# A two-block transformer kernel on one core: sums of squares for the norms, spread over DVE, ACT and TensorE in another way

## The chip, the cores and the metric

The kernel runs on 1 core of one Trainium2 chip. The time is device time in microseconds (us); of several runs the median is given. The engines are TensorE (PE in the profile; PEld are its weight loads), VectorE (DVE), ScalarE (ACT), GpSimd (POOL) and SyncE (SP, which issues the DMAs of the weights).

## The reference

A sequence of 512 tokens with 1024 channels goes through two blocks. What matters here are the RMS norms between the parts:

```python
def rmsnorm(x, g):
    xf = x.astype(jnp.float32)
    y = xf * lax.rsqrt(jnp.mean(xf * xf, axis=-1, keepdims=True) + RMS_EPS)
    return (y * g.astype(jnp.float32)).astype(x.dtype)

# first block, two layers (pooling mixer, then gated mixer "sgu")
x = x + g1 * mixer(modulate(rmsnorm(x, norm_mix_g[i]), sh1, sc1))
x = x + g2 * square(relu(modulate(rmsnorm(x, norm_mlp_g[i]), sh2, sc2) @ w1)) @ w2
x = rmsnorm(x, final_g)

# second block, one layer
h = rms_norm(x, norm_mix_pre)
proj = h @ w_in                          # q, k, v and the inputs of the recurrence
mix = concat(attention(q, k, v), rwkv7_time_mix(...)) @ w_out
x = x + rms_norm(mix, norm_mix_post)
f = conv_gated_ffn(rms_norm(x, norm_ffn_pre), w_ffn_up, conv_w, conv_b, w_ffn_down)
x = x + rms_norm(f, norm_ffn_post)
```

Inside `rwkv7_time_mix` the decays are `exp(-exp(w_log))` with `w_log` from `tanh(zw) @ w_decay_up`, and the rates of a are `sigmoid(a0 + za @ w_iclr_up)`.

## The kernel before

The activations lie transposed: channels on the 128 partitions in eight tiles (`xT[:, 0..7]`), the 512 tokens along the free axis. Every linear layer is worked off in slabs of 512 x 512 weights. DMA brings a slab to `raw`; ACT copies its rounded high part to `w_hi` (`split_to`, line 1140), DVE takes the low part `w_lo` as the difference (line 1568); TensorE makes 16 tile products of three matmuls each (`slab`, line 531). Two slabs are held at a time. The product of a group of slabs fills four PSUM banks, one for each tile of 128 outputs; a bank is evicted as soon as it is full, by DVE or ACT, while TensorE fills the next.

The order on each engine is that of its own program, written out by hand: `tensor_program`, `scalar_program`, `vector_program`, `gpsimd_program` and `sync_program`. They meet in counting semaphores. There is no planner.

A norm runs as follows. ACT squares the eight tiles (`square`, line 1158), each into one of four places of `squares`: tile 0 into place 3, the others in turn into places 0 to 2. DVE adds each to place 3 (`add_square`, line 1595), so seven additions make the sum over tiles. TensorE sums it over the partitions (`norm_mean`, line 542): for each 128 tokens the sum is loaded as the stationary operand, and one column of 1/1024 runs through it, so that the mean of each token comes to a partition of bank 4. ACT takes the root (`root`, line 1162), DVE the reciprocal and a diagonal matrix (`inverse_and_diagonal`, lines 1583 and 1585), TensorE spreads it over all partitions (`norm_spread`, line 547), and DVE and ACT scale the tiles and split them in high and low parts, for which the first slab of the next layer waits.

The norms are named after their place: `NORM_MIX0` before the pooling mixer (its additions are on POOL), `NORM_MLP0` before the first MLP, `NORM_MIX1` behind it, `NORM_MLP1` after `sgu_out`, `NORM_FINAL` after the second MLP, `NORM_POST` after `w_out`, `NORM_FFN` before the feed-forward, `NORM_LAST` behind it. Where squares come from a layer with two groups of output tiles, the additions of tiles 1 to 3 are made while the second group is multiplied, and those of tiles 4 to 7 after the last eviction. At `NORM_POST`, ACT evicts the banks to `mixed` (line 1502) and squares tiles 4 to 7 from there after the last of them. At `NORM_FFN` the squares are those of `xT` as DVE makes it, tile by tile, from `mixed` (lines 2201 and 2205); one addition stands in each step of that loop from the third on.

In the projection of the second block (`proj`, five pairs of slabs) other matmuls stand between the slabs. After the first slab of the second pair comes `decays` on TensorE (line 757), which waits for `first_copied`: a copy by ACT (line 1374) of the spread of `NORM_FINAL` out of bank 5. Four matmuls of the same shape follow later, `rates` (line 763).

## Time and profile before

| | |
|---|---|
| runs, us | 2003.49, 1999.51, 2000.14 (median 2000.14) |
| profiled execution, us | 2002.35, its span 2000.9 |
| mean granted TensorE clock in it | 0.941 of full speed |
| PE busy | 1825.2 us, 91% |
| PEld busy | 1473.2 us, 74% |
| DVE busy | 1052.0 us, 53% |
| ACT busy | 645.0 us, 32% |
| POOL busy | 82.5 us, 4% |

The span goes from the first to the last instruction of the profiled execution; the 1.45 us beside it lie around them. Busy shares of different engines overlap. TensorE's granted clock stands at one of two levels, 1.00 (2.4 GHz) or 0.50 (1.2 GHz); a stretch with both has a value between. An fp32 matmul leaves two records each of PE and PEld.

### The profile page before, as it was taken

What the parts mean: (1) busy time and instruction counts of PE and PEld (TensorE: products, weight loads), DVE (VectorE), ACT (ScalarE), POOL (GpSimd) and SP (SyncE); (2) the same over time, 40 slices, a digit from 0 to 9 for tenths busy, and PEclk for the clock granted to TensorE, in tenths of its full rate; (3) what the DMA queues carried; (4) which work ended last, traced back from release to release, by engine and by line L of the source; (5) the groups of instructions that cost most, each with busy time, mean ns of one, the idle gap of its engine ahead of it and who ended that gap; (6) DMA issues with size and microseconds to landing.
All of it is one profiled execution on the core that took longest, in us unless ns stands there. A gap on an engine that the chain in (4) does not pass through costs nothing.

```text
span 2000.9 us, 21459 instructions
## 1 busy us (share of the span) xinstructions
PE 1825.2 (91%) x8828; PEld 1473.2 (74%) x8828; DVE 1052.0 (53%) x1336; ACT 645.0 (32%) x796; POOL 82.5 (4%) x87
## 2 busy tenths in 40 slices
PE   4659999999896899999999989976599999999997
PEld 2238888888685688888886868855388888888885
DVE  4874675477426544234356574444565642456533
ACT  2123312322322243123244523332244431344412
POOL 2400010000000000000000101000000000000000
PEclk8769999999897899999998989987699999999997
DMA  9713474366230232323322240002123323232321
GB/s 356 275 64 105 143 236 151 102 209 222 74 105 9 76 105 87 104 88 102 105 90 69 85 100 4 4 1 66 40 85 105 100 90 105 84 105 91 100 84 42
DMA packets 124000, 208.55 MB, mean 104 GB/s; under 512 B 13965, under 2 KB 48421, under 8 KB 123904
## 3 DMA queue, kind: packets, MB, share of 16 engines
q1 hardware_dynamic: 115424, 174.94, 26.7%
q0 software_dynamic: 7808, 29.43, 4.4%
q10 hardware_dynamic: 672, 2.82, 0.4%
q8 instruction: 70, 1.15, 0.2%
q14 instruction: 26, 0.21, 0.0%
HBM read 204.01 MB, written 4.73 MB: 104 GB/s over the span
## 4 chain that ended last, share of the span: by engine, by line
PE 85%; DVE 10%; ACT 2%; DMA 1%; issue 1%; SPq 1%; DVEq 0%; ACTq 0%
PE bank L531 73%; DVE ada_acc L1643 2%; DMA ada_ring<-in_ada_w 1%; PE bank L878 1%; PE bank L547 1%; PE bank L861 1%; PE bank L841 1%; SPq L476 1%; PE bank L542 1%; DVE gT L1969 1%; DVE outer L1967 0%; PE bank L923 0%; PE bank L673 0%; PE bank L902 0%; PE bank L950 0%
## 5 line engine op out<-in xcount | busy, mean ns | idle before, releaser
L1568 DVE TENSOR_TENSOR w_lo<-raw,w_hi 128x2048 fp32r<-128x2048 f32 x138 | 316.2, 2292 | 533.0 <-ACT w_hi L1140 533.0
L1140 ACT ACTIVATE w_hi<-raw 128x2048 fp32r<-128x2048 f32 x138 | 263.8, 1912 | 632.7 <-PE bank L531 609.8
L531 PE MATMUL bank<-u_hi,w_hi 128*128 128x512 f32 x768 | 300.6, 391 | 0.8 <-DVE conv L2225 0.8
L531 PE MATMUL bank<-h_hi,w_hi 128*128 128x512 f32 x736 | 292.8, 398 | 7.9 <-DVE h_lo L1615 7.7
L531 PE MATMUL bank<-u_hi,w_lo 128*128 128x512 f32 x768 | 299.1, 389 | 0.0
L531 PE MATMUL bank<-u_lo,w_hi 128*128 128x512 f32 x768 | 298.9, 389 | 0.0
L531 PE MATMUL bank<-h_lo,w_hi 128*128 128x512 f32 x736 | 289.4, 393 | 0.0
L531 PE MATMUL bank<-h_hi,w_lo 128*128 128x512 f32 x736 | 289.2, 393 | 0.0
L531 PE MATMUL bank<-f_hi,w_hi 128*128 128x512 f32 x512 | 200.4, 391 | 2.4 <-DVE f_lo L1618 2.4
L531 PE MATMUL bank<-f_lo,w_hi 128*128 128x512 f32 x512 | 199.9, 391 | 0.0
L531 PE MATMUL bank<-f_hi,w_lo 128*128 128x512 f32 x512 | 199.8, 390 | 0.0
L531 PEld LDWEIGHTS bank<-h_hi,w_hi 128*128 128x128 f32 x736 | 139.9, 190 | 47.4 <-issue 15.1
L531 PEld LDWEIGHTS bank<-u_hi,w_hi 128*128 128x128 f32 x768 | 144.2, 188 | 31.1 <-DVE conv L2225 1.6
L531 PEld LDWEIGHTS bank<-u_hi,w_lo 128*128 128x128 f32 x768 | 144.2, 188 | 30.4
L531 PEld LDWEIGHTS bank<-u_lo,w_hi 128*128 128x128 f32 x768 | 144.2, 188 | 29.6
L531 PEld LDWEIGHTS bank<-h_hi,w_lo 128*128 128x128 f32 x736 | 140.0, 190 | 29.7
L531 PEld LDWEIGHTS bank<-h_lo,w_hi 128*128 128x128 f32 x736 | 140.3, 191 | 28.8 <-issue 0.5
L531 PEld LDWEIGHTS bank<-f_hi,w_hi 128*128 128x128 f32 x512 | 96.4, 188 | 25.3 <-issue 3.9
L531 PEld LDWEIGHTS bank<-f_hi,w_lo 128*128 128x128 f32 x512 | 96.5, 189 | 20.0
L531 PEld LDWEIGHTS bank<-f_lo,w_hi 128*128 128x128 f32 x512 | 96.6, 189 | 19.9
L1793 DVE SCALAR_TENSOR_TENSOR ada_acc<-ada_ring,c_act,ada_acc 128x256 f32<-128x256 f32 x168 | 81.4, 485 | 6.0
L1525 ACT ACTIVATE conv<-bank,vec 128x512 f32<-128x512 f32 x64 | 50.0, 781 | 104.7 <-PE bank L531 104.7
(351 smaller groups left out, 2040.3 us busy)
## 6 DMA issues: line engine op xcount, KB each, us to landing
raw<-in_mlp_w SPq DMA_DIRECT2D x128, 512.0 KB, 4.6
raw<-in_w_ffn_up SPq DMA_DIRECT2D x64, 512.0 KB, 4.4
ada_ring<-in_ada_w POOLq DMA_DIRECT2D x24, 1024.0 KB, 5.8
ada_ring<-in_ada_w SPq DMA_DIRECT2D x9, 2048.0 KB, 13.9
raw<-in_w_ffn_down SPq DMA_DIRECT2D x32, 512.0 KB, 4.4
raw<-in_w_in SPq DMA_DIRECT2D x20, 512.0 KB, 4.4
raw<-in_sgu_w_in SPq DMA_DIRECT2D x16, 512.0 KB, 4.9
x_rows<-in_ada_w SPq DMA_DIRECT2D x3, 2048.0 KB, 11.8
```

Of the source, the lines that this page charges most:

```text
L476: sy.dma_start(m.ada_slot(g), t["ada_w"][0, :, 512 * g:512 * g + 512] .rearrange("(k p) n -> p k n", p=P)).then_inc(sem(f"ada_in{g % ADA_R ...
L531: mm = te.matmul(bank[:, n], a, b, start=first and k == 0 and j == 0, stop=last and k == 3 and j == 2)
L542: mm = te.matmul(bank[:, 4, j:j + 1], total[:, P * j:P * j + P], m.mean_ones[:, 0:1], start=True, stop=True)
L547: te.matmul(m.rstd_bank, ones[:, :], m.rstd_diag[:, :, :].rearrange("p j t -> p (j t)"), start=True, stop=True).then_inc(sem("spread"), 1)
L841: mm = te.matmul(bank[:, b + i // 2, 256 * (i % 2) + j0:256 * (i % 2) + 256], m.qT[r0:r0 + 64, i, P * n:P * n + P], m.kT[r0:r0 + 64, P * n ...
L861: mm = te.matmul(bank[:, 7, 64 * i:64 * i + 64], m.p_t[:, q, i], m.v_rows[:, n - 1 + q, 64 * half:64 * half + 64], start=q == (n == 0), st ...
L878: mm = te.matmul(bank[:, b + hp, 256 * ii:256 * ii + 256], stationary[rr, i, tok], m.ar[rr, i, :, tok], start=True, stop=True)
L1140: se.activation(m.ring(s)[0], m.raw[:, slot], ACT.Copy).then_inc(sem("hi_made"), 1)
L1525: se.activation(m.conv[:, n], bank[:, n], ACT.Identity, scale=m.col("conv_w_2", 128 + place), bias=m.col("conv_b_2", place)).then_inc(sem( ...
L1568: ve.tensor_tensor(lo, m.raw[:, slot], hi.bitcast(F32), ALU.subtract).then_inc(sem("lo_made"), 1)
L1643: ve.scalar_tensor_tensor(out=a, in0=m.ada_slot(g)[:, k], scalar=m.c_act[:, k:k + 1], in1=a, op0=ALU.mult, op1=ALU.add).then_inc(sem("ada_ ...
L1793: ve.scalar_tensor_tensor(out=a, in0=m.ada1_ring[:, u % 2, kk], scalar=m.c_act[:, kk:kk + 1], in1=a, op0=ALU.mult, op1=ALU.add).then_inc(s ...
```

## The change

The program for each engine is changed by hand:

- After `NORM_MIX1`'s, `NORM_MLP1`'s and `NORM_LAST`'s layers, DVE adds the square of tile `o - 1` right behind the eviction of tile `o`, for tiles 5 to 7, and not all four additions after the last eviction.
- At these three and at `NORM_POST`, the square of tile 7 is no longer added by DVE. It lies in place 0, and `norm_mean` makes four more matmuls from it, which accumulate on the same four columns.
- At `NORM_POST`, ACT squares tiles 4 to 7 directly from their banks, each ahead of the copy that evicts it.
- At `NORM_FFN`, DVE makes no additions. ACT writes the eight squares to eight places, and `norm_mean_of_all` sums them on TensorE, four matmuls for each, which accumulate.
- On ACT, the copy that `first_copied` stands for moves ahead of the split of one slab.
- `NORM_MIX0`, `NORM_MLP0` and `NORM_FINAL` keep their seven additions; only the start flag of the mean's matmuls stands on the first of the four alone, at all norms.

```diff
@@ Python level
-ADDED_ON_DVE = (NORM_MLP0, NORM_MIX1, NORM_MLP1, NORM_FINAL, NORM_POST, NORM_FFN, NORM_LAST)
+ADDED_ON_DVE = (NORM_MLP0, NORM_MIX1, NORM_MLP1, NORM_FINAL, NORM_POST, NORM_LAST)
+LAST_APART = (NORM_MIX1, NORM_MLP1, NORM_POST, NORM_LAST)
+SUMMED_ON_PE = (NORM_FFN,)
+def additions(norm):
+    return 6 if norm in LAST_APART else 7
@@ tensor_program
-    def norm_mean(norm, total):
-        name, count = added(norm, 7)
+    def norm_mean(norm, squares):
+        name, count = added(norm, additions(norm))
         te.wait_ge(sem(name), count)
+        apart = norm in LAST_APART
         for j in range(4):
-            mm = te.matmul(bank[:, 4, j:j + 1], total[:, P * j:P * j + P], m.mean_ones[:, 0:1], start=True, stop=True)
+            mm = te.matmul(bank[:, 4, j:j + 1], squares[:, 3, P * j:P * j + P], m.mean_ones[:, 0:1], start=j == 0, stop=not apart,
+                           skip_group_check=True)
+        if apart:
+            te.wait_ge(sem("squared"), 8 * norm + 8)
+            for j in range(4):
+                mm = te.matmul(bank[:, 4, j:j + 1], squares[:, 0, P * j:P * j + P], m.mean_ones[:, 0:1], start=False, stop=True,
+                               skip_group_check=True)
+        mm.then_inc(sem("meaned"), 1)
+
+    def norm_mean_of_all(norm, squares):
+        for k in range(DT):
+            te.wait_ge(sem("squared"), 8 * norm + k + 1)
+            for j in range(4):
+                mm = te.matmul(bank[:, 4, j:j + 1], squares[:, k, P * j:P * j + P], m.mean_ones[:, 0:1], start=k == 0 and j == 0,
+                               stop=k == DT - 1, skip_group_check=True)
         mm.then_inc(sem("meaned"), 1)
...
-    norm_mean(NORM_POST, squares[:, 3])
+    norm_mean(NORM_POST, squares)
     norm_spread(NORM_POST)
-    norm_mean(NORM_FFN, squares[:, 3])
+    norm_mean_of_all(NORM_FFN, squares)
@@ scalar_program
     def square(norm, k, src, squares):
+        if norm in SUMMED_ON_PE:
+            se.activation(squares[:, k], src, ACT.Square).then_inc(sem("squared"), 1)
+            return
...
     normed_hi(range(4, 8))
-    split_to(first + 3)
     se.wait_ge(sem("spread"), NORM_FINAL + 1)
     se.activation(m.first_rstd, m.rstd_bank, ACT.Copy).then_inc(sem("first_copied"), 1)
+    split_to(first + 3)
     decays()
...
         for n in range(4):
             full(s + 1, group, n)
+            if g:
+                square(NORM_POST, 4 + n, bank[:, n], squares)
             se.activation(m.mixed[:, 4 * g + n], bank[:, n], ACT.Copy).then_inc(sem("act_emptied"), 1)
-    for o in range(4, 8):
-        emptied(GROUPS["w_out"] + 1, o - 4)
-        square(NORM_POST, o, m.mixed[:, o], squares)
@@ vector_program, mlp
                     if layer and half and g:
                         gained_lo(o)
-        for o in range(4, 8):
-            add_square(next_norm, o, sq)
-            if layer:
+                    elif half and g and n:
+                        add_square(next_norm, o - 1, sq)
+        if layer:
+            for o in range(4, 8):
+                add_square(next_norm, o, sq)
                 add_second_square(o)
@@ vector_program, after sgu_out
+            if g and n:
+                add_square(NORM_MLP1, o - 1, m.sq_c)
-    for o in range(4, 8):
-        add_square(NORM_MLP1, o, m.sq_c)
@@ vector_program, after w_out and before the feed-forward
-    for o in range(4, 8):
+    for o in range(4, 7):
         add_square(NORM_POST, o, squares)
...
         ve.tensor_tensor(m.xT[:, k], m.xT[:, k], m.mixed[:, k], ALU.add).then_inc(sem("x_mixed2"), 1)
-        if k >= 2:
-            add_square(NORM_FFN, k - 1, squares)
-    add_square(NORM_FFN, 7, squares)
@@ vector_program, after the last down projection
                     ve.tensor_tensor(m.f[:, o], m.f[:, o], bank[:, n], ALU.add).then_inc(sem("dve_emptied"), 1)
-    for o in range(4, 8):
-        add_square(NORM_LAST, o, m.conv)
+                    if g and n:
+                        add_square(NORM_LAST, o - 1, m.conv)
```

## Rows read from the trace of the kernel before

**Rows 1.** The page: the chain that ended last, shares by engine.
```profile
PE 85%; DVE 10%; ACT 2%; DMA 1%; issue 1%; SPq 1%; DVEq 0%; ACTq 0%
```

**Rows 2.** Timeline at the norm after `sgu_out` (start us, us, engine, line, op, tiles, count, [idle]).
```profile
682.69 0.75 DVE L1858 SCALAR_TENSOR_TENSOR xT<-bank,mod,xT 128x512 f32<-128x512 f32 x1 [1.97 <-PE bank L531]
683.36 3.07 DVE L1595 TENSOR_TENSOR sq_c<-sq_c 128x512 f32<-128x512 f32 x4
...
686.48 1.05 PE L542 MATMUL bank<-mean_ones,sq_c 128*128 128x1 f32 x8 [3.83 <-DVE sq_c L1595]
...
688.82 2.07 PE L547 MATMUL bank<-rstd_diag,ones 128*128 128x512 f32 x2 [1.29 <-DVE rstd_diag L1585]
```

**Rows 3.** Timeline at the norm after the first layer's MLP.
```profile
499.20 0.75 DVE L1761 SCALAR_TENSOR_TENSOR xT<-bank,mod,xT 128x512 f32<-128x512 f32 x1 [1.20 <-PE bank L531]
...
502.99 1.35 PE L542 MATMUL bank<-mean_ones,sq_b 128*128 128x1 f32 x8 [3.04 <-DVE sq_b L1595]
...
505.23 0.21 DVE L1803 TENSOR_TENSOR mod<-bank,vec 128x48 f32<-128x48 f32 x1 [2.30 <-PE bank L673]
```

**Rows 4.** Timeline at the norm after `w_out`.
```profile
1415.61 0.60 ACT L1502 ACTIVATE mixed<-bank 128x512 f32<-128x512 f32 x1 [2.12 <-PE bank L531]
...
1419.89 1.87 PE L542 MATMUL bank<-mean_ones,ar 128*128 128x1 f32 x8 [4.32 <-DVE ar L1595]
1421.80 0.26 ACT L1162 ACTIVATE rstd_rows<-bank,eps 128x4 f32<-128x4 f32 x1 [3.51 <-PE bank L542]
```

**Rows 5.** Timeline at the feed-forward's norm.
```profile
1425.16 0.75 DVE L2201 SCALAR_TENSOR_TENSOR mixed<-mixed,vec,bank 128x512 f32<-128x512 f32 x1 [2.17 <-PE bank L547]
...
1426.56 0.74 DVE L2201 SCALAR_TENSOR_TENSOR mixed<-mixed,vec,bank 128x512 f32<-128x512 f32 x1
1426.67 0.63 ACT L1158 ACTIVATE ar<-xT 128x512 f32<-128x512 f32 x1 [4.61 <-DVE xT L2205]
...
1442.69 0.26 ACT L1162 ACTIVATE rstd_rows<-bank,eps 128x4 f32<-128x4 f32 x1 [2.69 <-PE bank L542]
```

**Rows 6.** Timeline at the last norm.
```profile
1976.68 1.28 ACT L1162 ACT_TABLE_LOAD   x1
...
1978.38 1.87 PE L542 MATMUL bank<-mean_ones,conv 128*128 128x1 f32 x8 [3.77 <-DVE conv L1595]
```

**Rows 7.** Timeline around the decay matmuls.
```profile
1081.20 1.89 ACT L1140 ACTIVATE w_hi<-raw 128x2048 fp32r<-128x2048 f32 x1
...
1083.00 0.58 ACT L1374 ACTIVATE rstd_diag<-bank 128x512 f32<-128x512 f32 x1
1083.12 2.29 DVE L1568 TENSOR_TENSOR w_lo<-raw,w_hi 128x2048 fp32r<-128x2048 f32 x1 [1.04 <-ACT w_hi L1140]
...
1083.72 7.04 PE L757 MATMUL bank<-zT,lora 64*128 64x512 f32 x8 [2.95 <-ACT rstd_diag L1374]
...
1090.69 0.80 PE L531 MATMUL bank<-h_hi,w_hi 128*128 128x512 f32 x1
```

**Rows 8.** Line 542 in answer to its source: duration ns min/median/max, first and last start.
```profile
L542 PE MATMUL bank<-mean_ones,ar x16: 352/352/373, 1419.9 to 1442.3; 128*128 128x1 f32 x16
...
L542 PE MATMUL bank<-mean_ones,sq_c x8: 250/250/271, 686.5 to 687.3; 128*128 128x1 f32 x8
```

**Rows 9.** Stretches of TensorE: length, PE busy (records), granted clock, DMA share, GB/s.
```profile
686.48:687.57 1.09, 1.05 (x8) 1.00 0.00 0
1080.80:1083.70 2.90, 0.00 (x0) 1.00 0.04 7
1084.10:1094.20 10.10, 10.10 (x17) 0.51 0.36 119
1103.50:1107.10 3.60, 3.60 (x9) 1.00 0.63 241
1319.96:1323.90 3.94, 2.69 (x25) 1.00 0.02 4
1419.89:1421.76 1.87, 1.87 (x8) 0.50 0.00 0
```

More of the change, by code:

```diff
@@ L395, in added @@
         return "pool_added", 7 * ADDED_ON_POOL.index(norm) + k
-    return "dve_added", 7 * ADDED_ON_DVE.index(norm) + k
+    return "dve_added", sum(additions(n) for n in ADDED_ON_DVE[:ADDED_ON_DVE.index(norm)]) + k
 def slab_sources(t):
@@ L593, in tensor_program @@
     ada_row(1)
-    norm_mean(NORM_MIX0, m.pooled[:, 3])
+    norm_mean(NORM_MIX0, m.pooled)
     ada_sum(0)
@@ L664, in mlp @@
         if next_norm:
-            norm_mean(next_norm, sq[:, 3])
+            norm_mean(next_norm, sq)
     ada1 = {"summed": 0}
@@ L681, in tensor_program @@
     te.wait_ge(sem("mod_made"), 11)
-    norm_mean(NORM_MLP0, m.sq_b[:, 3])
+    norm_mean(NORM_MLP0, m.sq_b)
     mlp(0, NORM_MLP0, NORM_MIX1, m.u_hi, m.u_lo, m.sq_b, ada1_beside)
@@ L729, in tensor_program @@
     two_slabs("sgu_out", 2, m.g_hi, m.g_lo, gated, k_outer=True)
-    norm_mean(NORM_MLP1, m.sq_c[:, 3])
+    norm_mean(NORM_MLP1, m.sq_c)
     mlp(1, NORM_MLP1, None, m.u2_hi, m.u2_lo, m.sq_d)
     def two_means():
-        norm_mean(NORM_FINAL, m.sq_d[:, 3])
+        norm_mean(NORM_FINAL, m.sq_d)
         te.wait_ge(sem("second_added"), 7)
@@ L1116, in tensor_program @@
                      before_k if g == 0 else None, before_n, k_outer=g == 0 and k == 0)
-    norm_mean(NORM_LAST, m.conv[:, 3])
+    norm_mean(NORM_LAST, m.conv)
     norm_spread(NORM_LAST)
```

## The prediction

> **What bounds the kernel.** I read the chain that ended last first: 85% of it is TensorE [rows 1], which works off slabs of weights one behind the other. What can be won is therefore where TensorE stands still or runs at its low clock. The waits of TensorE and the timelines show such places at each RMS norm: a slab ends, the last output tile is evicted, squares are added one after the other on DVE, TensorE takes the mean, ACT the root, DVE the reciprocal and a diagonal, TensorE spreads it, and only then does the next slab start. Each instruction there is on the path. The reader is to see in [rows 2] that the last eviction starts at 682.69, that four additions of 3.07 us lie between it and the mean at 686.48, and that the spread starts at 688.82. The mean waits in the same way in [rows 3], [rows 4] and [rows 6], for 3.0, 4.3 and 3.8 us by the idle times in its rows. In [rows 7], TensorE has waited 2.95 us when it starts the decay matmuls.
>
> **The price of a mean.** A mean is four matmuls with one output column, eight records in the trace. At the high clock (1.00) they take 1.05 us, at the low one (0.50) 1.87 us [rows 9]; one record alone lasts 0.25 and 0.352 us [rows 8]. So the stream advances by (1.05 - 0.25)/7 = 0.114 us and (1.87 - 0.352)/7 = 0.217 us for each record. Sixteen records take 15 x 0.114 + 0.25 = 1.96 us at the high clock and 3.61 us at the low one.
>
> **Part 1, norms after the first MLP, after sgu_out and after the last down projection.** Additions of squares 4 to 6 move between the evictions, which are apart by four matmul tiles (1.97 us of waiting before one [rows 2]); one addition stays behind the last eviction. Square 7 isn't added: ACT makes it beside that addition (0.63 against 0.69 us), and TensorE sums it apart. Three additions leave the path, (3.07 - 0.69)/3 x 3 = 2.38 us, and eight records come, 8 x 0.114 = 0.91 us: 1.47 us at the high clock, 2.38 + 1.87 - 3.61 = 0.64 us at the low one. The interleaved additions themselves cost nothing, since TensorE waits for no bank there; were that cover gone, each would cost 0.69 us.
> After sgu_out the mean was at the high clock and starts earlier now: 1.4 us. After the first MLP the mean took 1.35 us [rows 3] (mixed clock) and would start 2.38 us earlier, at 500.61, and end at 502.57 in place of 504.34: 1.8 us; the column sums queued behind it on TensorE, for which DVE waits until 505.23, gain some tenths by the higher clock. I take 2.0. At the last norm the mean was at the low clock (1.87 us) [rows 6] and moves from 1978.38 to 1976.0; I expect the higher clock in most of it: 2.38 + 1.87 - 1.96 = 2.3, with 1.5 if both are alike. I take 2.0. The table load of 1.28 us follows the last square on ACT [rows 6], so it moves forward too and ends at about 1977.3, before the root at 1978.0.
>
> **Part 2, the norm after w_out.** ACT squares tiles 4 to 7 straight from the bank, ahead of the copy. The copy of tile 7 started at 1415.61 and the root at 1421.80 [rows 4]. Now square 7 starts at 1415.61 and ends at about 1416.24, additions 4 to 6 are long done, and TensorE takes the first four matmuls right behind the slab and the last four from 1416.29: the end is at 1417.4 and the root at 1417.5, 4.3 us earlier. The extra copy behind the square (0.60 us) ends at 1416.8, under the mean. The spread takes 2.07 us at the low clock [rows 2]; so little idle time lies before it now that it may still run at the high one, for half of that. I take 0.5 of it: 4.8 us, with 2.6 if both means fall to the low clock (3.61 - 1.96 less) and 5.3 at best.
>
> **Part 3, the feed-forward's norm.** From the first scaling at 1425.16 to the root at 1442.69 it took 17.53 us [rows 5]. DVE loses all seven additions, so its step for one tile falls to the 1.40 us between 1425.16 and 1426.56, where none stood. But TensorE gets 64 records in place of 8. The first can start when the first square is made: 1426.67 - 1425.16 + 0.63 + 0.05 = 2.2 us after the scaling. (0.05 us is the step from one engine to the next, as from the last addition's end at 686.43 to the mean at 686.48.) At the low clock the 64 take 63 x 0.217 + 0.35 = 14.0 us, so the root comes at 16.2 us: 1.3 us are won, and TensorE, not DVE, sets the end. At the high clock a tile's eight records (0.91 us) fit in DVE's step, and the root comes at 7 x 1.40 + 1.51 + 0.63 + 0.05 + 1.05 = 13.0 us: 4.5 us won. The clock was at 0.50 in the mean of [rows 9] that comes 3.4 us before this loop, and single-column matmuls with long pauses around them did not raise it there. I take 1.3.
> The Trainium skill, in "TensorE: Matmul & The Clock Gate", section "LDWEIGHTS (loading the stationary operand)", has the load of the stationary operand take its columns divided by 1.2, whatever the clock: an estimate from it is 107 ns for the 128 columns here, 0.85 us for a tile's eight. By that rule a tile's eight loads fit in DVE's step and Part 3 would come to 4.5 us and not 1.3. The records of [rows 8, 9] follow it at the high clock (0.114 us) but not at the low one (0.217 us).
>
> **Part 4, one copy on ACT moved in front of a weight split.** The decay matmuls need the copy at 1083.00, which stood behind a split of 1.89 us begun at 1081.20 [rows 7]. The copy now starts at 1081.20 and takes 0.58 us; the matmuls follow 0.14 us later, at 1081.92, 1.8 us earlier. The wait of 2.95 us falls to 1.15. In the trace the clock was still 1.00 in the idle 2.90 us and then 0.51 over the next 10.1 [rows 9]: the decay matmuls took 7.04 us, while the like ones of the rates, at the clock 1.00, took 3.6 us. Elsewhere a stretch of 3.94 us with 2.69 of work, the rest idle in one piece, stayed at 1.00 throughout [rows 9]. So I expect the high clock to be kept: matmuls until 1085.5. The split, now at 1081.8, and its low part of 2.29 us end at 1086.0, which is late next; the slab starts at 1086.05 in place of 1090.69 [rows 7], 4.65 us, and the 3.5 us of slab that ran at the low clock until 1094.2 take half: 1.75. Together 6.4 us; 1.8 if the clock is low from the first decay matmul on, 3.7 if it falls some 2 us into them. What follows until the blocks go out to DRAM is released by TensorE and shifts with it.
>
> **Sum.** 2.0 + 1.4 + 2.0 + 4.8 + 1.3 + 6.4 = 17.9 us. The profiled execution took 2002.35 us (span 2000.9), so it would be 1984.4; it lies 2.2 us above the median of the runs, and from 2000.14 the sum gives 1982.2. I forecast 1982.5. Within 0.2%, 4 us, this kernel can't be told from no change. Elsewhere the low clock only shifts with the work; where it begins and ends can add or take 2 us in all.
>
> **Rivals.**
> First, the clock falls at the decay matmuls all the same: they use 64 of 128 partitions, and the full stream of them did not raise the clock in [rows 9]. Against it: the rates' matmuls, of the same shape, kept it. Part 4 gives 1.8 to 3.7 us in place of 6.4: 1986. Chance 0.17.
> Second, TensorE keeps pace in the feed-forward's norm, by the high clock or because a load costs the same at both. Part 3 gives 4.5: 1979. Against it stand the 1.87 us at the low clock in [rows 9]; for it, that the stream is denser than any mean before. Chance 0.09. For it speaks also the Trainium skill's rule named above ("TensorE: Matmul & The Clock Gate", "LDWEIGHTS").
> Third, what Part 4 wins is swallowed before w_out, by the round trip through DRAM and DVE's inverses, if these are bound by something that does not shift: the chain has 10% of DVE [rows 1], a good part of it there. The sum falls to 11.5: 1988.5. Chance 0.07.
> Fourth, slower: matmuls that accumulate on the same four columns wait for one another. At 0.352 us a record [rows 8] Part 3 would take 64 x 0.352 + 2.2 = 24.7 us and lose 7, and the doubled means would give up about 6 more: 1996. If load and matmul don't overlap either, at 0.56 us or more a record, Part 3 alone loses 20.7 us and the kernel is over 0.2% slower, 2004 and up. The slab's matmuls accumulate on one bank without any such wait. Chance 0.02 for slower, 0.02 for 1996.
>
> **How the numbers follow.** My forecast, Parts 1 to 4 as summed, has 0.63; its own range is 1980 to 1985.5, from the clock's place and the bounds of Parts 1 and 2. The second rival ends the range below, the third above: 1978 to 1989.5 leaves out about 0.1 on paper, and I keep that for what I have not seen. Faster by over 0.2% is every case but the last: 0.95; within 0.2% 0.03; slower 0.02.
>
> **What would show it.** Right: at the four norms one addition or none between the last eviction and the mean; sixteen records there, of about 2 us; root after w_out 1.9 us behind the last slab; 64 records in a row of 0.217 us steps in the feed-forward's norm, with ACT's squares well ahead of them; decay matmuls of 3.6 us at the clock 1.00. Wrong: decay matmuls of 5 us or more; records in the feed-forward's norm at 0.114 us with pauses between tiles; an eviction of TensorE's banks that it waits for.

## The result, and the profile after

The changed kernel takes 1991.51 us (median of 6 runs, 1987.53 to 1992.4) against 1999.86 us for the kernel before beside it: a ratio of 0.995, 95% interval 0.9937 to 0.9963. That is 8.4 us, where 17.9 had been summed. Run again unaltered it took 1990.82 us against 2001.05, 10.2 us less. The profiled execution took 1990.98 us, its span 1989.6, so the spans of the two profiled executions lie 11.3 us apart. The chain that ended last has nearly the same shares as in [rows 1]:

```profile
PE 86%; DVE 9%; ACT 2%; DMA 2%; issue 1%; SPq 1%; DVEq 0%; ACTq 0%
```

The places that the change touches look much as forecast. The timeline at the norm after the first MLP, against [rows 3]:

```profile
500.01 0.74 DVE L1788 SCALAR_TENSOR_TENSOR xT<-bank,mod,xT 128x512 f32<-128x512 f32 x1
...
501.41 1.05 PE L553 MATMUL bank<-mean_ones,sq_b 128*128 128x1 f32 x8 [0.71 <-DVE sq_b L1622]
...
502.32 1.54 PE L558 MATMUL bank<-mean_ones,sq_b 128*128 128x1 f32 x8
...
504.75 0.21 DVE L1832 TENSOR_TENSOR mod<-bank,vec 128x48 f32<-128x48 f32 x1 [3.40 <-PE bank L698]
```

From the last eviction's start to the column sums' product it takes 4.74 us, where it took 6.03: 1.3 us, not 2.0, as the clock falls inside the mean (1.54 us for its second half, 1.05 for the first). After `sgu_out`, against [rows 2]:

```profile
681.99 0.75 DVE L1887 SCALAR_TENSOR_TENSOR xT<-bank,mod,xT 128x512 f32<-128x512 f32 x1 [1.37 <-PE bank L540]
...
683.40 1.05 PE L553 MATMUL bank<-mean_ones,sq_c 128*128 128x1 f32 x8 [1.44 <-DVE sq_c L1622]
...
684.31 1.03 PE L558 MATMUL bank<-mean_ones,sq_c 128*128 128x1 f32 x8
...
686.64 1.77 PE L572 MATMUL bank<-rstd_diag,ones 128*128 128x512 f32 x2 [1.29 <-DVE rstd_diag L1612]
```

Eviction to spread is 4.65 us, where it was 6.13; with the spread, 1.8 us are won. At the norm after `w_out`, against [rows 4], and in the feed-forward's norm, against [rows 5]:

```profile
1411.60 0.95 PE L553 MATMUL bank<-mean_ones,ar 128*128 128x1 f32 x8
1411.80 0.60 ACT L1186 ACTIVATE ar<-bank 128x512 f32<-128x512 f32 x1 [1.64 <-PE bank L540]
1412.29 0.59 ACT L1532 ACTIVATE mixed<-bank 128x512 f32<-128x512 f32 x1
...
1412.45 1.05 PE L558 MATMUL bank<-mean_ones,ar 128*128 128x1 f32 x8
1413.54 0.26 ACT L1190 ACTIVATE rstd_rows<-bank,eps 128x4 f32<-128x4 f32 x1 [0.66 <-PE bank L558]
...
1414.79 2.08 PE L572 MATMUL bank<-rstd_diag,ones 128*128 128x512 f32 x2 [1.29 <-DVE rstd_diag L1612]
1416.91 0.75 DVE L2230 SCALAR_TENSOR_TENSOR mixed<-mixed,vec,bank 128x512 f32<-128x512 f32 x1 [2.17 <-PE bank L572]
```
```profile
1428.10 0.63 ACT L1180 ACTIVATE ar<-xT 128x512 f32<-128x512 f32 x1 [0.75 <-DVE xT L2234]
1432.95 0.26 ACT L1190 ACTIVATE rstd_rows<-bank,eps 128x4 f32<-128x4 f32 x1 [4.22 <-PE bank L566]
```

From the start of ACT's first work on the last bank (now the square) to the root it is 1.74 us, where it was 6.19. In the feed-forward's norm the last square is done at 1428.73 and the root waits for TensorE until 1432.95: TensorE, at its low clock, sets the end, and from the first scaling to the root it is 16.04 us (forecast 16.2). The last norm, against [rows 6]; the clock is high in its mean now (1.05 and 1.03 us for eight records, where they took 1.87), and from the start of the last eviction to the root it is 3.3 us, where it was 5.6:

```profile
1967.10 1.05 PE L553 MATMUL bank<-mean_ones,conv 128*128 128x1 f32 x8 [1.38 <-DVE conv L1622]
1967.13 1.28 ACT L1190 ACT_TABLE_LOAD   x1
...
1968.02 1.03 PE L558 MATMUL bank<-mean_ones,conv 128*128 128x1 f32 x8
1969.09 0.26 ACT L1190 ACTIVATE rstd_rows<-bank,eps 128x4 f32<-128x4 f32 x1 [0.67 <-PE bank L558]
```

The decay matmuls, against [rows 7]:

```profile
1079.44 0.58 ACT L1401 ACTIVATE rstd_diag<-bank 128x512 f32<-128x512 f32 x1
...
1080.17 3.67 PE L782 MATMUL bank<-zT,lora 64*128 64x512 f32 x8 [1.16 <-ACT rstd_diag L1401]
...
1081.85 2.29 DVE L1595 TENSOR_TENSOR w_lo<-raw,w_hi 128x2048 fp32r<-128x2048 f32 x1 [1.52 <-ACT w_hi L1165]
...
1084.25 0.47 PE L540 MATMUL bank<-h_hi,w_hi 128*128 128x512 f32 x1 [0.41 <-issue]
```

The wait fell from 2.95 to 1.16 us and they kept the high clock in this execution. The places add up to about what the forecast had: 1.3 + 1.8 + 2.3 for Part 1, 4.4 for Part 2, 1.5 for Part 3 and 6.3 for Part 4 (from the final norm to the rates) make 17.6 us. What the whole lacks of that, at 11.3, has to be lost outside these places. Between these two traces, 3.2 us of it are in the key norms, 1.5 in the stretch from the keys' way back to `w_out`, and 1.4 before the final norm. The key norms are 16 matmuls with two columns (32 records), which start 24 us behind the decays' first. The windows from their first matmul to the first of the keys' way back (length; PE, PEld, DVE, ACT and POOL busy with records; granted clock; DMA share; GB/s), first in the changed kernel, then in the kernel before:

```profile
1104.58:1116.92 12.34, 12.34 (x58) 10.72 (x57) 4.05 (x4) 7.11 (x6) 0.23 (x1) 0.72 0.26 85
```
```profile
1112.64:1121.72 9.08, 9.08 (x58) 8.04 (x57) 4.05 (x4) 7.12 (x6) 0.00 (x0) 1.00 0.37 115
```

The same 58 records take 3.3 us more, with TensorE busy all the time, at a granted clock of 0.72 in place of 1.00.

### The profile page after: what moved, and what is told of

It reads as the page before. It is cut to its first block, busy times and chain, and to the rows that moved or that the text cites. A ratio compares the mean times of both kernels' runs of the same rounds, so it can differ in the third digit from the quotient of the medians.

```text
span 1989.6 us, 21610 instructions
## 1 busy us (share of the span) xinstructions
PE 1843.3 (93%) x8916; PEld 1490.5 (75%) x8916; DVE 1045.6 (53%) x1325; ACT 645.2 (32%) x796; POOL 82.9 (4%) x87
## 3 DMA queue, kind: packets, MB, share of 16 engines
q8 instruction: 71, 1.16, 0.2%
## 4 chain that ended last, share of the span: by engine, by line
PE 86%; DVE 9%; ACT 2%; DMA 2%; issue 1%; SPq 1%; DVEq 0%; ACTq 0%
PE bank L540 73%; DVE ada_acc L1670 2%; DMA ada_ring<-in_ada_w 1%; PE bank L903 1%; PE bank L572 1%; PE bank L566 1%; PE bank L886 1%; PE bank L866 1%; SPq L485 1%; DVE gT L1998 0%; DVE outer L1996 0%; PE bank L948 0%; PE bank L698 0%; PE bank L927 0%; PE bank L975 0%
```

## The experiments

Each ran in 4 to 12 executions beside the kernel before (its median 2001.05 to 2001.76 us). One kernel's executions scatter by 1 to 8 us, so a stage of one trace proves little, and stages are compared over many traces. The changed kernel did not run beside most of the variants, so "below" or "slower than the changed kernel" sets medians taken at different times against each other; its own two medians are 1991.51 and 1990.82 us. The stage table stands behind the experiments.

**The parts one by one.** `copy_behind` is the changed kernel without Part 4, `copy_alone` the kernel before with it alone:

```diff
-    se.wait_ge(sem("spread"), NORM_FINAL + 1)
-    se.activation(m.first_rstd, m.rstd_bank, ACT.Copy).then_inc(sem("first_copied"), 1)
     split_to(first + 3)
+    se.wait_ge(sem("spread"), NORM_FINAL + 1)
+    se.activation(m.first_rstd, m.rstd_bank, ACT.Copy).then_inc(sem("first_copied"), 1)
```

> The changed kernel with Part 4 taken back (the copy stands behind the split again). Theory A: Part 4 won its 6.4 us at its place (the decay matmuls took 3.67 us in the changed kernel, as forecast) and what is missing in the total was lost elsewhere, above all where the clock fell in the middle of the key-norm matmuls (line 797, 4.6 us instead of 3.5). Then this kernel's stretch from the mean of the first block's last norm to the rates' matmuls is 6.3 us longer, but whether the clock falls in the key-norm matmuls is open, and the total is 3 to 6.5 us above the changed kernel's, 1994.5 to 1998. Theory B: Part 4 wins little in the total, because the time is given back at the key norms whenever TensorE comes there without a low-clock stretch shortly before: total within 2 us of the changed kernel.

1993.69 us (1991.99 to 1997.73), ratio 0.9969 [0.9957, 0.998]: Part 4 is worth 2.2 us there by the medians, between the two theories. The interval overlaps with the changed kernel's.

> The kernel before with Part 4 alone. Theory A: 6.3 us shorter up to the rates; the total 3 to 6.5 us below before, 1993.5 to 1997, the lower figure if the key-norm matmuls keep the high clock. Theory B: within 2 us of before, with the key-norm matmuls at 4.5 us or more.

1997.38 us (1996.54 to 1999.28), 0.9985 [0.9976, 0.9994]: worth 3.8 us alone, not 6.4. That is just short of theory A's 1993.5 to 1997, though its trace is 6.3 us shorter up to the rates.

`ffn_on_dve` has the feed-forward's norm added on DVE, with its last tile taken apart like the others:

```diff
...
-LAST_APART = (NORM_MIX1, NORM_MLP1, NORM_POST, NORM_LAST)
-SUMMED_ON_PE = (NORM_FFN,)
+LAST_APART = (NORM_MIX1, NORM_MLP1, NORM_POST, NORM_FFN, NORM_LAST)
+SUMMED_ON_PE = ()
...
+        if k >= 2:
+            add_square(NORM_FFN, k - 1, squares)
```

> The changed kernel with the feed-forward norm's squares added on DVE again, the last one taken by TensorE apart as at the other norms. By the rows: last square at 1439.37 + 0.63 after a first scaling at 1425.16, then sixteen records at the low clock, 3.61 us: 18.3 us from the first scaling to the root, where the changed kernel has 16.0 (1416.91 to 1432.95). So 2.3 us slower than the changed kernel. Rival: TensorE's stream of 64 records brings the clock up sooner for the slab behind it; then the loss is 4 us and the low stretch after the norm is longer here.

1994.12 us (1991.67 to 1996.02), 0.9966 [0.9954, 0.9979]: 2.6 us slower than the changed kernel, near the 2.3 expected. This compares two ways of summing; Part 3 by itself was never timed.

`post_alone` is the kernel before with Part 2 alone (the diff of that norm on ACT and DVE, and `LAST_APART = (NORM_POST,)`).

> The kernel before with Part 2 alone: in the norm behind w_out ScalarE squares each tile of the second half straight from its bank ahead of the copy, and the last tile is summed apart. The forecast gave it 4.8 us, and the traces show the stretch from the w_out slabs to this norm's spread 4.4 to 5.0 us shorter in all kernels that have it. Theory A (this reaches the end, as no slab but 20 us of a norm stands right behind it): 1996 to 1997 us. Theory B (the clock's low stretch behind it starts earlier and ends as late, and takes a part): 1997.5 to 1999.5 us.

1997.2 us (1995.77 to 1999.06), 0.998 [0.9972, 0.9989]: 3.9 us, most of the 4.8.

`part1_undone` takes Part 1 out of the changed kernel:

```diff
-LAST_APART = (NORM_MIX1, NORM_MLP1, NORM_POST, NORM_LAST)
+LAST_APART = (NORM_POST,)
...
-            if g and n:
-                add_square(NORM_MLP1, o - 1, m.sq_c)
+    for o in range(4, 8):
+        add_square(NORM_MLP1, o, m.sq_c)
```

and likewise at the two other norms.

> The changed kernel with the additions of the squares back behind the last eviction, and no tile taken apart, in the norms of the first mix, the first feed-forward and the last norm (the forecast's Part 1); the other parts stay. At the places themselves the changed kernel's trace won 1.3, 1.8 and 2.3 us, 5.4 in all. Theory A (these reach the end but for what the low clock takes in the slabs behind, which was 0.7 us behind the first feed-forward's norm and 0.8 near the start): 3.5 to 4.5 us slower than the changed kernel, near 1995.5 us. Theory B (they reach the end whole): 5.4 us slower, near 1997 us. Theory C (the clock takes more than half of them back): 1 to 2.5 us slower.

1990.89 us (1989.66 to 1992.1), 0.9949 [0.9937, 0.9962], against 1991.51 with it. All three theories fall: taking Part 1 out costs nothing that can be measured.

**Is it chance?** The changed kernel again, and Part 1 alone on the kernel before.

> The changed kernel once more, unaltered, beside the next three: a second trace and more times of the same instructions. Undoing Part 1 in the changed kernel cost nothing that shows in the total (1990.89 against 1991.51 us), though its profile shows 1.6 us lost up to the final norm and 1.6 us lost behind the second feed-forward; it made them good by 1.6 us in the key norms and 3.8 us between the inverse and the w_out slabs, where no instruction differs. Theory A (those 5.4 us are chance, by where the clock falls in one execution): this second trace of the changed kernel differs from the first by some microseconds in these same stretches (12.3 us from the key norms to the keys' way back, 180.2 us from the inverse's end to w_out), and by under 0.6 us from the first slab to the final norm and behind the feed-forward's norm. Theory B (Part 1 itself shifts the phase and brings the loss): the second trace shows the same lengths as the first in all of them, and the median stays at 1991.5.

1990.82 us (1989.55 to 1993.96), 0.9951 [0.9939, 0.9964]. From the first slab to the final norm it has the first trace's length (912.8 and 912.7 us), and so in the key norms (12.3). From the keys' way back to `w_out` it is 245.7 us, where it was 249.6: that stretch differs by chance, as theory A has it, but the key norms do not. The decays differ by chance too: the clock, high throughout in the first trace, falls in them in this one. From the first decay matmul to the slab behind, and from there to the rates, first in the changed kernel's first trace, then in this one (length, PE busy with records, clock, DMA share, GB/s):

```profile
1080.17:1084.25 4.08, 3.67 (x9) 1.00 0.26 66
1084.25:1095.41 11.16, 11.16 (x49) 1.00 0.30 94
```
```profile
1080.09:1084.67 4.58, 4.54 (x9) 0.79 0.17 59
1084.67:1098.04 13.37, 13.37 (x50) 0.82 0.34 105
```

> The kernel before with Part 1 alone: the additions between the evictions and the last tile taken apart, in the norms of the first mix, the first feed-forward and the last norm. Nothing else differs from before. Theory A (the forecast's sum, 5.3 us): 1995 to 1996 us. Theory B (what the profiles show stage by stage, 1.6 us up to the final norm and 1.6 us behind the last feed-forward slab, reaches the end): 1997 to 1998 us. Theory C (as its undoing in the changed kernel had it: nothing): within 1 us of the kernel before, 2000 to 2002 us.

2000.95 us (1997.32 to 2004.81), 0.9998 [0.9989, 1.0007]: theory C, nothing.

**Which of Part 1's norms?** `part1_first` has it in the two first norms alone, `part1_last` in the last alone; the kernel before and Part 1 alone ran once more beside them.

> The kernel before with Part 1 in the norms of the first mix and the first feed-forward alone. Their own stages are 0.9 us shorter in the mean of the traces (from the first slab to the final norm). Theory A (they shift the work behind them so that the clock falls for longer in the key norms, 2 to 4 us): slower than before by 1 to 3 us, 2002 to 2004 us, with 71.5 us or more from the final norm to the keys' way back. Theory B (that was chance): 0.9 us faster, near 2000 us, which a comparison of these runs can't tell from no difference, and the stretch at 69 to 71 us.

2003.6 us (1999.27 to 2007.62), 1.0016 [1.0008, 1.0025]: 2.5 us **slower** than before: theory A by its time. Its trace, of a faster execution (2002.4 us), shows gains and losses that cancel: the final norm comes 1.8 us sooner behind the first slab (912.2 against 914.0 in the mean of the two traces of before), the decays are 1.7 us shorter, the key norms 3.2 us longer. From the final norm to the keys' way back it has 70.8 us, where theory A had 71.5 or more.

> The kernel before with Part 1 in the last norm alone. Behind it stand only its own scaling and the output, so nothing can take back what it wins; the traces show 1.6 to 2.3 us from the feed-forward's slab to the end. Theory A and B alike: 1.6 to 2.3 us faster than before, near 1999 us. If it comes out at no difference, the stage lengths of single traces are no measure at all.

1998.58 us (1996.82 to 2001.73), 0.9987 [0.9979, 0.9996]: 2.5 us faster.

> The kernel before, unaltered, for a second trace beside the others. Theory A (the kernels without Part 1 keep the clock up in the key norms, or lose it briefly): the stretch from the final norm to the keys' way back at 69 to 71 us again. Theory B (chance): anything from 69 to 73 us. The median against the kernel before is 0 within 1 us.

2001.87 us (1999.07 to 2002.56), 1.0004 [0.9995, 1.0012], with 9.1 us in the key norms once more. Two medians of the same kernel, taken side by side, lie 0.75 us apart here.

> The kernel before with Part 1 alone, unaltered, for a second trace. Theory A: the stretch from the final norm to the keys' way back at 72 to 73 us again, and the total within 1 us of before. Theory B (chance): the stretch anywhere from 69 to 73 us, and a median that moves with it, down to 1998 us.

1998.82 us (1997.02 to 2003.66), 0.9992 [0.9984, 1.0001]: 2.3 us faster this time, more than theory A had, though its trace again shows 12.3 us in the key norms and 72.4 to the keys' way back. The two medians of this kernel differ by 2.1 us; Part 1 alone is worth between 0 and 2.3. It is only 0.2 us slower than `part1_last`, which ran beside it, where the loss of `part1_first` would make it 2.5 slower. The windows of the key norms, first in `part1_first`, then in `part1_last`:

```profile
1108.93:1121.22 12.29, 12.29 (x57) 10.71 (x56) 4.05 (x4) 7.12 (x6) 0.23 (x1) 0.72 0.25 85
```
```profile
1110.02:1120.68 10.66, 10.66 (x57) 9.20 (x56) 4.05 (x4) 7.11 (x6) 0.24 (x1) 0.84 0.32 98
```

**The key norms in four parts.** In `keys_apart` (on the changed kernel) and `before_keys_apart` their matmuls stand four at a time between the slab's:

```diff
...
+            def after_k(n, kk):
+                if n == 2:
+                    key_norms_part(kk)
...
```

> The changed kernel with the 16 key-norm matmuls in four parts of four, each behind one quarter of the third tile of the slab instead of all together behind its second tile. If the clock fell because weight loads with two output columns filled a stretch of 3.5 us with hardly a streamed column, it stays at 1.00 now, the following slab runs at its full rate, and the total is about 3.2 us below the changed kernel, 1988 to 1988.5. If the fall has another cause (the idle time before the decays, a time of its own), the total is the same within 1 us and the low-clock stretch is still there.

1990.37 us (1986.23 to 1991.26), 0.9947 [0.9934, 0.9959]: 1.1 us less, which these runs can't tell from nothing, and not the 3.2 expected. At the place the gain is there: from the rates to the keys' way back its trace has 18.4 us, against 21.5 in all eight traces with Part 1 in the two first norms and the key norms in one piece. Most of these 3.1 us did not reach the end.

> The kernel before with the 16 matmuls of the key norms issued in four parts between the slab's, and nothing else. In the profile of the kernel before the clock did not fall in the key norms; in that of the changed kernel and two variants it did. Theory A (the fall is as frequent in the kernel before, and that profile was the exception): about 3 us faster than before, near 1997 us. Theory B (the old order of work keeps the clock up there, and the change brought the fall): no difference, 2000 us within 1 us, and then 3 us of the missing gain are the change's own doing. A value in the middle means that the clock falls there in some of the executions of the kernel before.

2001.49 us (1999.3 to 2003.77), 1.0003 [0.9994, 1.0012]: no gain. Theory B: the kernel before keeps its clock there, and has nothing to win (18.3 us from the rates to the keys' way back as it stands, 18.4 in four parts).

`copy_first_keys_apart` has the copy ahead of the last of the norm's own tiles, too.

```diff
-    normed_hi(range(4, 8))
+    normed_hi(range(4, 7))
     se.wait_ge(sem("spread"), NORM_FINAL + 1)
     se.activation(m.first_rstd, m.rstd_bank, ACT.Copy).then_inc(sem("first_copied"), 1)
+    normed_hi((7,))
     split_to(first + 3)
```

> The changed kernel with two moves that keep TensorE from idling or streaming narrow matmuls between the final mix's norm and the decays' use: ScalarE's copy of the first norm's scale goes ahead of the last of the norm's own tiles instead of behind it, so that the decay matmuls start where the slab before them ends (the copy cost 1.16 us of idle time ahead of them after the change), and the 16 matmuls of the key norms are issued in four parts between the matmuls of the slab. Theory A (what the change won was partly given back because the clock fell in these places: 3.3 us in the key norms, 2.7 us behind the decays in those executions where it falls there): the decays start within 0.3 us of the slab's end, the granted clock stays at its high level from the final mix's norm to the keys' way back, that stretch is 3 to 5 us shorter than in the changed kernel, and the total is 3 to 5 us below it, about 1986 to 1988 us. Theory B (low-clock stretches come in about the same number whatever is moved, and one that is kept off here comes later): the total stays within 1 us of the changed kernel's, and the low-clock time between the inverse and the w_out slabs grows by what is won here.

1987.12 us (1985.79 to 1989.58), 0.993 [0.9916, 0.9943]: theory A by its time, 4.4 us below the changed kernel. Its trace keeps the high clock in the key norms, but not everywhere: the slab behind the decays had 0.87.

**Wide columns.** `ffn_wide` sums the feed-forward's norm with the ones as weights and 512 moving columns of squares. The mean stands in every partition, and neither diagonal nor spread is needed:

```diff
-            for j in range(4):
-                mm = te.matmul(bank[:, 4, j:j + 1], squares[:, k, P * j:P * j + P], m.mean_ones[:, 0:1], ...)
+            mm = te.matmul(bank[:, 4], m.mean_ones[:, :], squares[:, k], start=k == 0, stop=k == DT - 1)
...
-    norm_spread(NORM_FFN)
...
```

> The changed kernel with the feed-forward's norm summed on TensorE as eight matmuls with the ones as weights and the squares as 512 moving columns, instead of 32 (64 records) with the squares as weights and one moving column; the mean then stands in every partition, so that the spread over a diagonal goes, and ScalarE's root and VectorE's reciprocal work on 128x512 instead of 128x4. Theory A (the sum keeps ScalarE's pace, and wide columns keep TensorE's clock up into the slab behind): the stretch from the norm before to this norm's end falls by 1 to 3 us and the slab behind begins at the high clock, 2 to 5 us below the changed kernel in all. Theory B (the reciprocal of 128x512 costs as much as spread, diagonal and small root together, and the clock falls in the waits anyway): within 1 us of the changed kernel. A slow reciprocal (several us) would make it slower.

1987.52 us (1985.21 to 1990.23), 0.9932 [0.992, 0.9945], 4.0 us below the changed kernel: theory A by its time. From `w_out` to the feed-forward's slab it is 2.4 us shorter in the traces (69.8 against 72.2 us); but the slab behind does not begin at the high clock, as theory A had it: it runs at the low one for 4.9 us, where it was 6.1. Its timeline:

```profile
1426.02 0.63 ACT L1177 ACTIVATE ar<-xT 128x512 f32<-128x512 f32 x1 [0.75 <-DVE xT L2234]
...
1426.70 1.12 PE L565 MATMUL bank<-ar,mean_ones 128*128 128x512 f32 x2 [0.26 <-ACT ar L1177]
1427.86 0.69 ACT L1535 ACTIVATE rstd_diag<-bank,eps 128x512 f32<-128x512 f32 x1 [1.22 <-PE bank L565]
1428.58 3.35 DVE L2236 RECIPROCAL rstd_diag<-rstd_diag 128x512 f32<-128x512 f32 x1 [2.60 <-ACT rstd_diag L1535]
```

TensorE follows 0.05 us behind this last square (0.63 us from 1426.02). Against the changed kernel it gives up 3.35 us for a reciprocal of 128x512, and saves the queue of narrow matmuls, the diagonal and the spread.

**All three together,** `all_best`, twice, and once with Part 1 undone in the two first norms.

> The three edits that were faster than the changed kernel, together: the copy of the first norm's scale ahead of the last of the norm's own tiles, the key norms in four parts between the slab's matmuls (1987.12 us with both) and the feed-forward's norm summed with wide columns (1987.52 us alone). If they add up: 4.4 and 4.0 us below the changed kernel's 1991.51, so about 1983 us. If both only win by a luckier clock, which can be won once: about 1987 us.

1984.25 us (1982.69 to 1986.47), 0.9916 [0.9902, 0.9929], and with its repeat the fastest kernel of the study. The gains nearly add up (7.3 us of 4.4 + 4.0).

> Its pair: the kernel with the three further edits, unaltered, on the same chip. Both theories: 1984.25 us within 1 us, and 8.5 us from the key norms' first matmul to the keys' way back.

1984.21 us (1983.22 to 1985.32), 0.9912 [0.9899, 0.9926].

> The kernel with all three further edits (key norms apart, the copy ahead of the norm's last tile, the wide sum; 1984.25 us), with Part 1 undone in the norms of the first mix and the first feed-forward. Theory A (the loss by Part 1's two first norms comes only through the key norms, which this kernel no longer has in one piece): its own stages make it 0.7 to 1.2 us slower than its pair, near 1985 us. Theory B (the loss is in the phase of the clock and comes elsewhere too): it is 1 to 2.5 us faster than its pair, near 1982 us, and the fastest kernel so far.

1984.75 us (1984.31 to 1985.65), 0.9916 [0.9903, 0.993]. Where the key norms are apart, undoing Part 1 in the two first norms no longer gains; it costs 0.5 us, within the noise. That is nearer to theory A (0.7 to 1.2 us slower) than to theory B (1 to 2.5 us faster). From the key norms' first matmul to the keys' way back all three traces have 8.5 us, at the high clock.

**Stage lengths** in us, from starts in each kernel's timeline. "Key norms" is their first matmul to the keys' way back; where they stand in four parts it starts 0.7 us later in the slab, so that 8.5 us there stand for 9.2 of the others; "decays to rates" is the first decay matmul to the first of the rates.

| traces | first slab to final norm | decays to rates | key norms | final norm to keys' way back |
|---|---|---|---|---|
| before, before_again | 914.4, 913.6 | 19.7, 19.6 | 9.1, 9.1 | 69.2, 69.2 |
| post_alone, part1_last | 913.2, 912.0 | 19.4, 19.4 | 10.7, 10.7 | 70.6, 70.6 |
| part1_alone, its repeat | 912.7, 910.6 | 19.7, 19.6 | 12.3, 12.3 | 72.5, 72.4 |
| part1_first, copy_behind | 912.2, 912.9 | 17.9, 19.6 | 12.3, 12.3 | 70.8, 72.4 |
| copy_alone, part1_undone | 913.1, 914.5 | 15.1, 15.2 | 10.6, 10.7 | 64.5, 64.5 |
| after, after_again | 912.7, 912.8 | 15.2, 17.9 | 12.3, 12.3 | 66.2, 68.9 |
| ffn_on_dve, ffn_wide | 912.7, 910.9 | 17.9, 17.9 | 12.3, 12.3 | 68.9, 68.9 |
| keys_apart, copy_first_keys_apart | 912.1, 913.9 | 18.0, 17.5 | 8.5, 8.5 | 65.8, 64.1 |

The eight traces with Part 1 in the two first norms and the key norms in one piece have 12.3 us in them, the six without it 9.1 to 10.7. No trace breaks this. In the traces with 9.1 us the clock keeps its high level there, and in those with 12.3 us it is low for twice as long as in those with 10.7.

## Why the prediction was wrong

**The step that failed** is the one behind the sum: "Elsewhere the low clock only shifts with the work; where it begins and ends can add or take 2 us in all." No run shows this sentence, and no row stood behind it; the places that the change touches won nearly what was forecast, and more than those 2 us were given back in low-clock stretches behind them. Two terms suffer from it, Part 1 and Part 4.

**Part 1** was put at 2.0 + 1.4 + 2.0 = 5.4 us. Split in two, the last norm's share is worth 2.5 us in the times and 1.5 to 2.3 in the traces (from the feed-forward's slab to the end, 552.5 us without it, 550.2 to 551.0 with it, but 551.8 in `ffn_wide`), as forecast. The share of the two first norms, 3.4 in the forecast, was no gain in any comparison: a loss of 2.5 us timed alone, of 0.2 and 2.4 by Part 1 alone less its last norm, and of 2.5 to 3.2 by undoing Part 1 in the changed kernel (against its two medians). The traces show a part of that. The 1.3 and 1.8 us won at the places shrink to 0.9 by the final norm (913.4 us is the mean over all 8 traces without it, 912.5 over the 12 with it, which reach from 910.6 to 914.7, so that the 0.9 is uncertain by about half of it). One reason can be seen after `sgu_out`: the clock comes up no sooner behind the last eviction's start (15.2 us in the changed kernel, 15.5 before; 14.8 to 15.5 in 17 of the 20 traces, with Part 1 and without), and a slab that starts earlier runs more of its matmuls at the low one. The windows of TensorE from the slab's start (length, PE busy with records, clock, DMA share, GB/s) in the changed kernel and in the kernel before:

```profile
690.95:697.20 6.25, 6.25 (x13) 0.50 0.00 1
```
```profile
693.44:698.00 4.56, 4.56 (x10) 0.50 0.01 2
```

The slab starts 2.5 us earlier, but 1.7 us more of it runs at half speed, so 0.8 us are given back. Then the key norms take 12.28 us in place of 10.13 (the mean of the six): 2.1 us lost where nothing was changed. 2.1 less 0.9 is a loss of 1.2 us, of the 2.5 measured (the interval reaches from 1.6 to 5); the rest is open. That the loss goes through the key norms fits the kernel where they are apart: there, undoing Part 1 in the two first norms gained nothing. It is not proven: in `keys_apart` the 3.1 us won back at the place came to 1.1 at the end. What is shown is that the low clock in the key norms is longer with Part 1 in the two first norms in every trace, and that these two norms bring no time. Why the clock falls there for longer with Part 1, the runs don't tell; Part 1 changes no instruction there, only when the work arrives.

**Part 4** was put at 6.4 us with the high clock kept, 3.7 with it falling some 2 us into the decays; the expectation that it would be kept ("So I expect the high clock to be kept") is the step that failed here. From the final norm to the rates it took 50.9 us before (31.2 + 19.7), and 50.6 to 50.9 in seven of the eight other traces with the copy behind the split (49.2 in part1_first). With the copy ahead, three traces have 44.6 (29.5 + 15.1: after, copy_alone, part1_undone), 6.3 won, and four have 47.4 (after_again, ffn_on_dve, ffn_wide, keys_apart), 3.5 won. Both sizes were right, and the high clock was kept in three of these seven traces; the first rival, at 0.17, had it in the others. The timed worth, 3.8 alone and 2.2 in the changed kernel, is nearer to the lower of the two. But the trace of `copy_alone` itself won 6.3 us up to the rates and gave 1.6 back in the key norms (10.6 us against 9.1), so a fall at the decays is not all of it.

**Part 2** was right but for its last term: 6.19 - 1.74 = 4.45 us at the root (forecast 4.3). The spread took 2.08 us, so the 0.5 for a higher clock in it did not come. 3.9 of the 4.8 reached the end.

**Part 3** was right at its place, in its mechanism too. One answer of the trace:

```profile
L566 PE MATMUL bank<-mean_ones,ar x64: 352/352/373, 1419.1 to 1432.6; 128*128 128x1 f32 x64
```

64 records from 1419.1 to 1432.6 make 0.214 us each, at a granted clock of 0.50; TensorE lagged behind ACT by 4.2 us, and 1.5 us were won from 17.53 to 16.04 (forecast 1.3). The Trainium skill ("TensorE: Matmul & The Clock Gate", section "LDWEIGHTS (loading the stationary operand)") gives the load's time as the columns divided by 1.2 and names no clock for it: by an estimate from that, 107 ns a load, and TensorE keeping pace. The trace disagrees at the low clock. The second rival falls by the same 0.214 us. Nor did the accumulating matmuls wait for one another: the fourth rival had 0.352 us a record (and of its worst case, 64 x 0.56 + 2.2 - 17.5 is 20.5, not 20.7). The third rival's time, 1988.5, was nearest to the result, but not by its mechanism: with the copy alone, the stretch up to the keys' way back is 4.7 us shorter (64.5 against 69.2) and the whole 3.8. From the keys' way back to `w_out`, where the round trip through DRAM and the inverses lie, the 11 traces with the copy ahead have 248.6 us in the mean and the 9 with it behind 247.6; the traces of one kernel differ there by up to 4.2 us, so the 1 us that could be put down to that rival is not clear of chance.

**The sum by what was measured:** Part 1 alone 0.1 and 2.3, 1.2 in the mean; Part 2 3.9; Part 3 1.5 (by its stage, not timed); Part 4 3.8: 10.4 us, against the 8.4 and 10.2 measured. Part 1 is short by 4.2, Part 4 by 2.6, Part 2 by 0.9; together 7.7 of the 17.9. The first result is 9.5 us short of the sum; some 2 us of that stand in no part.

## What to carry to other kernels

Time won at a place in front of a slab is not time won at the end when the clock is low there: price the slab behind it at the clock it will start in, and look down the stream for TensorE work with few columns, which an earlier arrival can tip into the low clock, as in the key norms here. An edit of 1 to 3 us on such a kernel is judged by timing it alone and by undoing it, and by the same stage over many traces, never by one pair of traces. Three further edits gave 7 us more here than the change had: the copy another place forward, narrow matmuls spread between wide ones (1.1 us alone, within the noise), and a sum turned round so that the data moves in 512 columns (4.0 us).

## What the runs showed of the hardware

- The granted clock can fall while TensorE has no idle time at all: in the key norms, with two columns to a matmul, PE was busy 12.34 of 12.34 us at a clock of 0.72.
- Nor did it rise in the 13.81 us in which TensorE worked off the 64 one-column records of the feed-forward's norm without a pause: it was 0.50 from 1419.10 to 1432.91. In `ffn_wide`, whose sum of the same squares moves 512 columns and begins at 1417.01, it was 1.00 from 1423.00 to the end of the sum at 1427.82.
- Records of one column behind a load of 128 columns step by 0.114 us at the high clock and by 0.214 us at the low one.
- A stage without any difference in its instructions, between the keys' way back and `w_out`, took 249.6 us in one trace of the changed kernel and 245.7 in the other; its mean granted clock was 0.91 and 0.93.
- DVE's reciprocal of 128x512 took 3.35 us, where its product of two 128x512 tensors takes 0.69.
